# Weight buffers at 0 instead of 128 modulo 256 bytes, with three small constants ahead of them

## The reference

```
for l in range(DEPTH):
    h = rmsnorm(x, mix_norm[l]);  p = h @ w_in[l]
    mix = concat([mla(p, w_uq, w_ukv), pool(p, w_pool), sg(p, w_s)])
    x = x + mix @ w_o[l]
    h = rmsnorm(x, ffn_norm[l])
    x = x + (silu(h @ w_gate[l]) * (h @ w_up[l])) @ w_down[l]
```

```
for l in range(DEPTH):
    sh1, sc1, g1, sh2, sc2, g2 = split(silu(c) @ ada_w[l] + ada_b[l], 6)
    y_ctx, y_lat = mixer_ab(...) if l % 2 == 0 else mixer_c(...)
    x = x + g1 * rmsnorm(y_lat, norm_g[l, 1])
    x = x + g2 * rmsnorm(swiglu(modulate(x, ...), ffn_w_in[l], ffn_w_out[l]), norm_g[l, 3])
    # and the same for the context, but for the last layer
```

## Time and profile before

| | before |
|---|---|
| median of the runs | 2998.71 us |
| profiled execution | 3003.56 us |
| its span | 3001.7 us |
| mean granted TensorE clock | 0.988 |
| PE busy | 2939.2 us (98%), 16850 matmuls |
| PEld busy | 2472.5 us (82%) |
| DVE busy | 1824.3 us (61%) |
| ACT busy | 1266.1 us (42%) |
| POOL busy | 1308.7 us (44%) |
| DMA | 108 GB/s mean |

### The profile page before, as it was taken

How to read it: one execution, slowest core, us unless ns; L and a number is a source line. 1 busy time by engine, 2 the same in 40 slices (tenths; PEclk the granted TensorE clock), 3 DMA queues, 4 the chain that set the end, 5 groups by cost and what they waited for, 6 DMA issues and landing times.

```text
span 3001.7 us, 43067 instructions
## 1 busy us (share of the span) xinstructions
PE 2939.2 (98%) x16850; PEld 2472.5 (82%) x16850; DVE 1824.3 (61%) x3001; ACT 1266.1 (42%) x2026; POOL 1308.7 (44%) x687
## 2 busy tenths in 40 slices
PE   8999999999999999999999999999999999999999
PEld 7668888786688888778888998888787788889998
DVE  5656777856563553655337877666775667564455
ACT  4643222246454333225336555542222435454445
POOL 4323444532276334333444554454444430166665
PEclk9999999999999999999999999999999999999999
DMA  7224554522245323223333343445554220113332
GB/s 136 67 64 123 171 176 146 178 65 73 77 132 150 91 71 90 80 64 107 118 105 99 110 120 103 141 126 182 168 175 134 93 71 15 38 58 110 106 106 78
DMA packets 468697, 323.92 MB, mean 108 GB/s; under 512 B 90264, under 2 KB 435488, under 8 KB 467984
## 3 DMA queue, kind: packets, MB, share of 16 engines
q1 hardware_dynamic: 463728, 309.55, 35.1%
q0 software_dynamic: 2112, 5.32, 0.6%
q10 hardware_dynamic: 2656, 6.30, 0.6%
HBM read 315.85 MB, written 5.24 MB: 107 GB/s over the span
## 4 chain that ended last, share of the span: by engine, by line
PE 88%; DVE 7%; ACT 2%; POOL 2%; issue 1%; DMA 1%; POOLq 0%; DVEq 0%; ACTq 0%
PE G L3350 13%; PE G L3359 10%; PE G L3360 10%; PE G L3364 10%; PE G L3606 4%; PE G L3607 4%; PE G L3611 4%; PE G L3627 2%; PE G L3631 2%; PE G L3628 2%; PE G L3674 1%; PE G L3670 1%; PE G L3669 1%; PE G L4687 1%; POOL WL L844 1%; PE G L3379 1%
## 5 line engine op out<-in xcount | busy, mean ns | idle before, releaser
L844 POOL TENSOR_TENSOR WL<-raw,WH 128x1024 fp32r<-128x1024 f32 (+2 forms) x454 | 1051.5, 2338 | 1495.2 <-ACT WH L925 1495.2
L925 ACT ACTIVATE WH<-raw 128x1024 fp32r<-128x1024 f32 (+2 forms) x454 | 431.8, 999 | 474.5 <-PE G L3611 314.1
L3359 PE MATMUL G<-hH,WH 128*128 128x512 f32 x1216 | 476.9, 392 | 0.7 <-ACT xtok L1783 0.7
L3360 PE MATMUL G<-hL,WH 128*128 128x512 f32 x1216 | 473.6, 389 | 0.0
L1997 DVE SCALAR_TENSOR_TENSOR acc<-adaw,cvec,acc 128x512 f32<-128x512 f32 x280 | 285.8, 1073 | 4.2
L3364 PE MATMUL G<-hH,WL 128*128 128x512 f32 x1216 | 287.9, 389 | 0.0
L3359 PEld LDWEIGHTS G<-hH,WH 128*128 128x128 f32 x1216 | 228.2, 188 | 52.7 <-issue 3.3
L3364 PEld LDWEIGHTS G<-hH,WL 128*128 128x128 f32 x1216 | 228.2, 188 | 47.4
L3360 PEld LDWEIGHTS G<-hL,WH 128*128 128x128 f32 x1216 | 228.3, 188 | 46.6
L2026 DVE TENSOR_TENSOR FH<-silu,G 128x512 fp32r<-128x512 f32 x44 | 30.2, 687 | 233.7 <-PE G L3364 178.1
L896 POOL TENSOR_TENSOR WL<-raw,WH 128x512 fp32r<-128x512 f32 x101 | 129.4, 1297 | 79.7 <-ACT WH L1048 79.5
(11 more groups left out here) (887 smaller groups left out, 6910.7 us busy)
## 6 DMA issues: line engine op xcount, KB each, us to landing
raw<-ffn_w_in_in SPq DMA_DIRECT2D x264, 256.0 KB, 3.4
adaw<-ada_w_in SPq DMA_DIRECT2D x48, 1024.0 KB, 5.2
raw<-ab_w_in_in SPq DMA_DIRECT2D x128, 256.0 KB, 3.0
raw<-ffn_w_out_in SPq DMA_DIRECT2D x96, 256.0 KB, 3.0
raw<-w_gate_in SPq DMA_DIRECT2D x88, 256.0 KB, 3.3
raw<-w_up_in SPq DMA_DIRECT2D x88, 256.0 KB, 3.4
raw<-w_down_in SPq DMA_DIRECT2D x64, 256.0 KB, 2.8
raw<-w_in_in SPq DMA_DIRECT2D x40, 256.0 KB, 3.5
```

The source lines that it names most:

```text
L844: nc.gpsimd.tensor_tensor(low(c)[:, cut], raw[c % 2][:, cut], high(c)[:, cut].bitcast(F32), ALU.subtract)\
L925: nc.scalar.activation(high(c)[:, cut], raw[c % 2][:, cut], ACT.Copy).then_inc(weights_hi, 1)
L3359: mm(dst, view(high(c), k), xh, start=(k == 0 and not (joint and i)), stop=False)
L3360: mm(dst, view(high(c), k), xl, start=False, stop=False)
```

## The change

The three constants cvec (64 bytes), squared_x (32) and lbs (32) move from behind the last weight buffer to the front of the first. Together they are 128 bytes. So WH0, WH1, WL0 and WL1, and the small constants between them (ncol, eps, g_mix, g_ffn, g_final, rope_cols, g_q, g_kv, g_pool, conv, g_ab), begin 128 bytes later: WH0 at 82176, WH1 at 90624, WL0 at 99072, WL1 at 107520, all at 0 modulo 256, and at column 16 that is 64. From lbn on every buffer is where it was, and so is everything ahead. The instructions of every engine and their order are the same as before.

```diff
         raw = [keep(f"raw{s}", [P, SLOT]) for s in range(2)]
+        cvec, squared_x, lbs = keep("cvec", [P, KD, 2]), keep("squared_x", [P, 2, 4]), keep("lbs", [P, 2, HA])
         WH0 = keep("WH0", [P, SLOT + SIDE], F32R)
         ncol, eps = keep("ncol", [P, 40]), keep("eps", [P, 1])
         WH1 = keep("WH1", [P, SLOT + SIDE], F32R)
...
         WL1 = keep("WL1", [P, SLOT + SIDE], F32R)
-        cvec, squared_x, lbs, lbn = keep("cvec", [P, KD, 2]), keep("squared_x", [P, 2, 4]), keep("lbs", [P, 2, HA]), keep("lbn", [P, 2, HA])
+        lbn = keep("lbn", [P, 2, HA])
         dec = keep("dec", [P, 2, 4])
```

## The result

The changed kernel takes 3041.5 us, the median of 4 runs (3039.97 to 3043.03), against 2997.97 us of the kernel before, the median of 4 runs at the same time. The ratio is 1.0142, with a 95% interval of 1.0124 to 1.0160: 43.5 us slower. The forecast was 3035 us.

What follows compares the result with a forecast made beforehand. PE's matmul stream was taken to bound the kernel, its time being number times pace. Terms 33.8 + 3.6 - 1.5 = 35.9 us, on the median of 2998.71, gave 3035 us, range 2985 to 3058.

Steps and rivals of the forecast that it cites:

- The bound and the place: Whole kernel: one long stream of matmuls on PE, whose pace changes with the addresses; other engines cost 0 us.
- 512 columns, 128 to 0: 6768 matmuls of 512 columns, weights moving from 128 to 0 modulo 256: 5.0 ns each, 33.8 us slower, ends 0 and 45.1.
- a stream just started: 8 steps from 309.31 to 311.15 us, after a stop, at 230 ns each: 3.3 ns over the usual pace.
- the price of 64 bytes: Last down projection, weights at 192 instead of 128: 233.3 against 226.7 ns, 6.7 ns a matmul, taken as upper bound.
- 256 columns of the last feed forward: Last gate and up projection, 1596 matmuls, weights from 192 to 64: 3.6 us slower, ends 0 and 7.2.
- The context's streams: 256-column matmuls of the context's passes, which show both paces before the change: taken at 0 us.
- The last down projection: 528 matmuls of 512 columns, weights from 192 to 64: taken at 0, could gain 3.5 us or lose as much.
- Moving weights: 672 matmuls of 256 columns with weights as moving operand, 128 to 0: from 120 to 118 ns, a gain of 1.5 us.
- The small constants, ScalarE and GpSimd at 0: Constants read as scalars, and the engines that write the weights: no cost from the new addresses, 0 us.
- nothing moves: Rival: pace depends on the distance modulo 128 only, so no matmul changes, 2999 us; chance 0.39.
- A pace below the present one: Rival: 6768 matmuls of 512 columns run at 220 ns and give back 45.1 us, 2954 us; chance 0.13.
- Twice the price: Rival: 512-column matmuls pay 6.7 ns once per 256 columns, 240 ns each, 90 us more, 3089 us; chance 0.05.

Runs made afterwards that it cites:

- The sweep: A program of its own, TensorE alone, 32 equal fp32r matmuls per pair of tile and row addresses: 512 columns took 226.7 ns at equal addresses modulo 256, 232.5 at 128 bytes apart.
- the third program: A program of its own: streams of 24 fp32r matmuls of 256 columns behind differing first matmuls, three times over; 117.9 ns behind 448 columns, 113.3 behind 384.
- the second sweep: A program of its own: rows of equal matmuls with tiles taken in turn, other widths and types; tiles at 128 and 0 in turn took 233.3 ns each.

## Why the prediction was right

**The bound and the place: right.** The whole change is in PE's pace. The other engines' durations stay, and all of PE's steps outside the named kinds took 0.4 us more together.

**512 columns, 128 to 0: direction right, size right with luck.** I took 5.0 ns, half way between a stream just started and the price of 64 bytes. The sweep has 5.8 ns, the chain's run of 144 has 5.7, and over the 7065 matmuls of this kind off the lower clock it is 5.1. Neither of the two rows has a distance of 128, and nothing tied the price to their middle; slower (0.48) and no change (0.39) were also near to each other. That a stream needs some steps before it is at 226.7 ns is borne out by the sweep; that its reads are out of step meanwhile is not shown. The term was 2.2 us short, most of it for the count: the listed groups (6768) leave out 216 of L3350, the 96 of L3879 and the attention's 96. The means differ by line, from 6.1 ns at L3360 (before L3359) to 0.1 and 1.4 ns in two profiles at L3377, which I have not explained.

**256 columns of the last feed forward: sign right, size off.** I took half of 4.5 ns for 1596 matmuls. It was all or little by the profile: 8.5 us in three of four profiles with this distance, 1.5 us in the fourth. **The context's streams, taken at 0, failed:** they cost 3.0 to 4.2 us. That both paces occurred there was no reason for 0, since the share of the short one was some 2700 of 3700 starts over both kinds of stream and had room to fall (some 240 after).

**The last down projection: mis-sized.** Taken at 0, it gave 2.2 us of the 3.5 us that the bound allowed: distance -64 has 229 ns, not 233.5. (Its 528 steps alone; the one step ahead of the last gate and up, at 2680 us, was 0.6 us shorter too and stands with the others.) That 64 bytes one way and 64 the other differ by 4.7 ns at 512 columns is what none of the rows of before showed.

**Moving weights: the step's reason failed, at a small price.** I had used 118 ns, seen at the distance of -64; at 128 it is 118.7 to 120.1, so the run of 96 stayed at 11.5 us where the sign named in the prediction was 11.3, and the sum over the 672 was -0.1 instead of -1.5 us.

**The small constants, ScalarE and GpSimd at 0: right.** Other constants in their place changed nothing beside the spread in the last gate and up.

The terms off 512 columns were forecast at +2.1 and measured +10.3 in the changed kernel's profile, the 512 at 33.8 and 36.0. So the forecast of 3035 us was 6.5 us low, and that the two profiles differ by 36.5 us, so near to the forecast's 35.9, is luck: the clock's 9.7 us the other way hide what the 256-column terms lacked. The rivals: *nothing moves* needed a period of 128 bytes, and the period is 256. *A pace below the present one* fell because distance 0 is the best for 512 columns of all eight measured. *Twice the price* does not occur. The rule of the Trainium skill (SBUF — State Buffer, "Who interferes with whom"), that TensorE's two read ports are independent and that it never waits on anyone, does not hold for fp32r in these runs: 226.7 to 233.9 ns by nothing but the distance. For bf16 (215.8 ns) and plain fp32 (429.2 ns a pass) the second sweep agrees with it, at one pace each for all starts.

What stays open: why the distance counts, why only in fp32r and only at the full clock, whether the spread in the last gate and up is the execution's or the chip's, and why the last gate and up came out differently in two executions of one kernel, where the third program repeated its paces in every turn; the kernel has waits and clock stretches ahead of it, and which of them decides was not tried.

## What to carry to other kernels

In a kernel bound by fp32r matmuls, lay the stationary tiles and the moving rows of 512 columns at the same address modulo 256 bytes, all of them, since a single odd tile slows its neighbour too; a sweep of two dozen pairs of addresses in one launch gives the table by which its 512-column streams are priced. The 256-column streams have two paces at one distance, so for them the table gives bounds only. Buffers laid one after the other hide such a dependence: three small constants of 128 bytes, laid ahead of the weights, cost 1.4%. Before the difference of two profiles is put down to an edit, subtract one from the other matmul by matmul: here up to 7 us were one long stream's pace and up to 10 us the clock.

## What the runs showed of the hardware

- fp32r matmuls of 512 columns run at 226.7 ns at distance 0, 228.8 at -64 and 232.5 to 233.9 at the six others; at 384 columns 173.4 to 176.7, at 128 columns 111.7 at all four tried. At the lower clock the distance costs nothing: 427 ns for 512 columns at 0, 128 and -64, 213 ns for 256.
- fp32r at 256 columns has two steady paces, 113.3 and 117.8 ns, at one and the same pair of addresses, set in the third program by what ran before and kept for up to 503 matmuls in a row. Distance 0, the best for 512 columns, is with 120.0 the worst here, together with 128 and 160.
- Both the tile in use and the one being loaded count: tiles in turn at distance 0 and 128 give 233.3 ns a step, at 0 and -64 229.9, at 0 and +64 230.0.
- bf16 (215.8 ns) and plain fp32 (429.2 ns a pass) do not care.
- The lower clock's stretches differ between executions of one kernel. The two profiles of the kernel before had a mean of 0.988 and the changed kernel's two 0.993, but over all recorded executions both kernels lie between 0.988 and 0.993, with no link to the addresses that these runs could show.
